# A convolutional decoder trunk on eight cores: the width-31 convolution computed for even and odd tokens at once

## The reference

```
h   = RMSNorm(x)
a_val, a_gate, z_a, gb, gc, hb, z_b = split(h @ w_in)          # 7 x 1024 columns
u   = a_val * sigmoid(a_gate)
ca  = causal depthwise conv, 31 taps, over u, + bias
ca  = LayerNorm of ca over the 128 channels of each of 8 heads
y_a = silu(ca) * silu(z_a)
v   = gc * hb
y_b = gb * (causal depthwise conv, 3 taps, over v) * silu(z_b)
x   = x + concat(y_a, y_b) @ w_out
```

## Time and profile before

| | us |
|---|---|
| median of 3 runs (1307.68 to 1352.38) | 1310.99 |
| the profiled execution | 1308.93 |
| span of its slowest core (core 2) | 1307.4 |
| spans of all eight cores | 1301.4 to 1307.4 |
| TensorE busy on it | 1220.8 |
| VectorE busy | 755.4 |
| ScalarE busy | 526.5 |
| GpSimd busy | 238.0 |

### The profile page before, as it was taken

How to read it: one execution, slowest core, us unless ns; L and a number is a source line. 1 busy time by engine, 2 the same in 40 slices (tenths; PEclk the granted TensorE clock), 3 DMA queues, 4 the chain that set the end, 5 groups by cost and what they waited for, 6 DMA issues and landing times.

```text
span 1307.4 us, 24848 instructions; the slowest of 8 cores (1301.4 to 1307.4 us)
## 1 busy us (share of the span) xinstructions
PE 1220.8 (93%) x8618; PEld 649.5 (50%) x8618; DVE 755.4 (58%) x1407; ACT 526.5 (40%) x764; POOL 238.0 (18%) x340
## 2 busy tenths in 40 slices
PE   4799999999899999999889999999999999999993
PEld 1355555555445555555445555544544555555541
DVE  2644456345666666667844445634476566666686
ACT  4677643767201101113537674367632111011252
POOL 0233323243010000000003333214230100100000
PEclk9999999999999999999999999999999999999997
DMA  9945431656143215230335553256441330422127
GB/s 245 197 92 107 104 73 37 126 113 119 17 96 55 34 26 92 34 52 13 41 78 123 101 105 72 51 106 125 88 49 24 52 49 8 65 33 33 17 107 168
DMA packets 89258, 102.09 MB, mean 78 GB/s; under 512 B 17008, under 2 KB 70384, under 8 KB 89072
## 3 DMA queue, kind: packets, MB, share of 16 engines
q0 software_dynamic: 20736, 37.76, 20.4%
q1 hardware_dynamic: 67584, 58.67, 18.5%
q10 hardware_dynamic: 816, 4.08, 0.9%
HBM read 92.41 MB, written 13.37 MB: 81 GB/s over the span
## 4 chain that ended last, share of the span: by engine, by line
PE 76%; DVE 6%; ACT 6%; issue 4%; DMA 4%; POOL 2%; SPq 1%; DVEq 0%; ACTq 0%; POOLq 0%
PE ps L327 66%; PE ps L442 7%; ACT sq L346 3%; DMA rep<-ubuf 2%; DVE x_sb L393 2%; PE ps L455 1%; DVE x_sb L379 1%; DMA x_sb<-xT 1%; PE ps L335 1%; POOL sq L425 1%; SPq L541 1%; PE ps L353 1%; DVE h_sb L371 1%; ACT L471 1%; DVE acc L665 1%
## 5 line engine op out<-in xcount | busy, mean ns | idle before, releaser
L327 PE MATMUL ps<-h_sb,wsl 128*128 128x424 bf16 (+1 forms) x4400 | 819.2, 342 | 2.0 <-ACT th_t L549 1.3
L327 PEld LDWEIGHTS ps<-h_sb,wsl 128*128 128x128 bf16 x4400 | 426.1, 98 | 363.9 <-issue 19.9
L327 PE MATMUL ps<-y_sb,wsl 128*128 128x424 bf16 (+1 forms) x1280 | 237.2, 342 | 15.9 <-DVE x_sb L393 15.9
L309 POOL DMA_DIRECT2D wsl<-w_in_r x112 | 60.1, 540 | 720.7 <-PE ps L327 507.8
L393 DVE TENSOR_TENSOR x_sb<-x_sb,ps 128x424 f32<-128x424 f32 (+1 forms) x320 | 175.4, 589 | 19.0 <-PE ps L327 8.8
L327 PEld LDWEIGHTS ps<-y_sb,wsl 128*128 128x128 bf16 x1280 | 123.9, 98 | 123.1 <-issue 22.7
L631 ACT ACTIVATE sz_t<-ps 128x424 f32<-128x424 f32 (+1 forms) x80 | 41.9, 523 | 303.4 <-PE ps L327 281.5
L556 DVE SCALAR_TENSOR_TENSOR ubuf<-th_t,ps 128x424 bf16<-128x424 f32 (+1 forms) x80 | 46.5, 583 | 180.5 <-PE ps L327 134.9
L442 PE MATMUL ps<-rep,wc 128*32 128x424 bf16 (+1 forms) x2560 | 119.7, 338 | 9.8 <-DMA rep<-ubuf 9.8
L665 DVE SCALAR_TENSOR_TENSOR acc<-ubuf,cw_b_sb,acc 128x424 f32<-128x424 bf16 (+1 forms) x192 | 112.8, 588 | 20.4 <-DVE acc L662 0.5
L647 DVE TENSOR_TENSOR ubuf<-ps,th_t 128x424 bf16<-128x424 f32 (+1 forms) x80 | 46.9, 586 | 130.5 <-PE ps L327 124.8
(11 more groups left out here) (50 smaller groups left out, 707.5 us busy)
## 6 DMA issues: line engine op xcount, KB each, us to landing
rep<-ubuf SPq DMA_DIRECT2D x256, 113.0 KB, 2.9
wsl<-w_in_r POOLq DMA_DIRECT2D x112, 256.0 KB, 5.3
wsl<-w_out_r POOLq DMA_DIRECT2D x32, 256.0 KB, 5.3
x_sb<-xT SPq DMA_DIRECT2D x16, 424.0 KB, 13.2
y_fm<-x_sb SPq DMA_DIRECT2D x16, 424.0 KB, 2.7
rep<-ubuf SPq DMA_DIRECT2D x64, 95.0 KB, 2.5
hista<-hist_a SPq DMA_DIRECT2D x16, 255.5 KB, 4.4
oa_copy<-sa_orig ACTq DMA_DIRECT2D x2, 1664.0 KB, 11.2
```

The lines of the kernel that those rows point to most:

```text
L309: P.op("pool", (lambda e, i=i, s=s: e.dma_start(out=wsl[:, s, :], in_=wseq[i])), reads=list(gate), writes=[w_r[s]], chan=ch_w[s], name=f"w ...
L327: ins = e.matmul(bank(bk, n), lhsT=l_, rhs=r_, start=(i == 0), stop=(i == len(pairs) - 1))
```

## The change

The tokens are reordered ahead of the launch: block 0 holds the even and block 1 the odd tokens of the first 848, blocks 2 and 3 those of the next 848, and block 4 the even, then the odd ones of its 352 prompt tokens, then the decode tokens. `ubuf` has a row of even and a row of odd tokens.

A convolution is now made for a group: blocks 0 and 1, blocks 2 and 3, or block 4 alone. `rep` has eight tiles; a tile's 128 rows are 16 channels x 2 phases x 4 shifts, and a matmul of 32 columns gives 16 channels x 2 phases. `a_copy` still issues four DMAs for each of blocks 0 to 3, now each from 128 partitions to 16, and eight for block 4. `st_conv` does a group in two banks (h = 0, 1), four passes each, over 424 columns (176 for block 4), and then casts both banks. `st_mean` takes channels and phases apart again and takes the mean away: two matmuls on `cb` with `um` for each block, four for block 4. `ones_n` is gone.

The order is changed too. `pipe` goes by the block number b: the group of blocks 0 and 1 is convolved in step 3 (banks 4 and 5), that of blocks 2 and 3 in step 0 of the next head (banks 4 and 5), block 4 in step 2 of the next head (banks 6 and 7). Their Ln and Exp come in steps 4 and 1; those of block 4 go with step 4. The output block of head 4 of group A comes one step later, the last in head 5. In group B the taps and the product of blocks 0 to 3 wait for the next step (`b_pend`), `out_norm(b - 2)` stands inside `b_step(b)` from b = 2 on, and the output blocks 3 and 4 of heads 3 and 7 follow `b_step(4)`. `rep` has two buffers (four before), `rstd_t` three and shared with the RMSNorm's, `sz_t` six with fixed places. `um` is one more load at the start, the taps of layer 1 are loaded in group B of layer 0, and the returned rows of u and v of the prompt are written in two pieces.

```diff
+HP = 16
+HQ = NPL // 2
+QN = SEQ // 2
...
+NM = 4
+NT = 8
+RW = BW + 4 * (NM - 1)
+NR = 2
...
+    ubuf = sb("ubuf", [128, 2, UQ], BF16)
     vbuf = ubuf
+    vsam = sb("vsam", [128, VSW], BF16)
...
+    rep = sb("rep", [128, NR, NT, RW], BF16)
     wsl = sb("wsl", [128, NW, 1024], BF16)
-    wc = sb("wc", [128, 2, 4 * NG, 32], BF16)
+    wc = sb("wc", [128, 2, NM * NT, 32], BF16)
+    um = sb("um_sb", [128, 4, 128], BF16)
...
+    def st_conv(gp, banks):
+        ms, rp, n = gp["j"] % 2, gp["rep"], gp["n"]
+        gp["bd"] = banks
+        for h in range(2):
+            def fn(e, h=h):
+                ins = None
+                for m in range(NM):
+                    for q in range(4):
+                        t = 4 * h + q
+                        off = 4 * (NM - 1 - m)
+                        ins = e.matmul(psum[32 * q:32 * q + 32, banks[h], 0:n], lhsT=wc[:, ms, NM * t + m, :], rhs=rep[:, rp, t, off:off + n],
+                                       start=(m == 0), stop=(m == NM - 1), tile_position=(0, 32 * q), skip_group_check=True)
+                return ins
+            P.op("pe", fn, reads=[wc_r[ms], rep_r[rp]], writes=[bank_r[banks[h]]])
+        for h in range(2):
+            P.op("dve", (lambda e, h=h: e.tensor_copy(cb[:, h, 0:n], bank(banks[h], n))), reads=[bank_r[banks[h]]], writes=[cb_r[h]])
+        for i, s in enumerate(gp["sts"]):
+            s["bd"] = banks[i]
+
+    def st_mean(gp, i):
+        s, n = gp["sts"][i], gp["n"]
+        bd, single = s["bd"], len(gp["sts"]) == 1
+        nb = BLOCKS[s["b"]][1]
 
         def fn(e):
             ins = None
-            for m in range(NG):
-                for q in range(4):
-                    w = wc[:, ms, 4 * m + q, :]
-                    ins = e.matmul(psum[32 * q:32 * q + 32, bd, 0:npr], lhsT=w, rhs=rep[:, rp, q, 4 * m:4 * m + npr],
-                                   start=(m == 0), stop=False, tile_position=(0, 32 * q), skip_group_check=True)
+            for p in ((0, 1) if single else (i,)):
+                c = n * p if single else 0
+                for h in range(2):
+                    ins = e.matmul(psum[:, bd, c:c + n], lhsT=um[:, 2 * h + p, :], rhs=cb[:, h, 0:n],
+                                   start=(h == 0 and c == 0), stop=(h == 1), skip_group_check=True)
+            if single:
+                ins = e.matmul(psum[:, bd, NPL:nb], lhsT=cmat16[:], rhs=cbs[:], start=False, stop=True, skip_group_check=True)
             return ins
...
+    def st_var_mm(s, bk):
+        nb = BLOCKS[s["b"]][1]
+        mm_group(bk, nb, [(ones_v[:], d2[:, s["d2"], 0:nb])], reads=[d2_r[s["d2"]], ones_r])
+        s["vb"] = bk
+
+    def st_rstd(pair, single):
+        ops = []
+        if pair:
+            vb, n = pair[0]["vb"], BLOCKS[pair[0]["b"]][1]
+            for t, s in enumerate(pair):
+                s["rstd"], s["rstd_r"] = rstd_t[:, t, 0:n], rstd_r[t]
+            ops.append((rstd_t[:, 0:2, 0:n], psum[:, vb:vb + 2, 0:n], [bank_r[vb], bank_r[vb + 1]], rstd_r[0:2]))
+        for s in single:
+            nb = BLOCKS[s["b"]][1]
+            s["rstd"], s["rstd_r"] = rstd_t[:, 2, 0:nb], rstd_r[2]
+            ops.append((rstd_t[:, 2, 0:nb], bank(s["vb"], nb), [bank_r[s["vb"]]], [rstd_r[2]]))
+        for o, i, rd, wr in ops:
+            P.op("act", (lambda e, o=o, i=i: e.activation(out=o, in_=i, func=AF.Ln, bias=LN_EPS)), reads=rd, writes=wr)
+        for o, i, rd, wr in ops:
+            P.op("act", (lambda e, o=o: e.activation(out=o, in_=o, func=AF.Exp, scale=-0.5)), reads=wr, writes=wr)
...
+    q_conv, q_y, hold = [], [], []
+    cur = {}
+
+    def pipe(at, b):
+        if at == 0:
+            gp = None
+            if q_conv and q_conv[0]["at"] == b:
+                gp = cur["g"] = q_conv.pop(0)
+                st_conv(gp, (6, 7) if b == 2 else (4, 5))
+            if b % 2 == 0:
+                while q_y:
+                    st_y(q_y.pop(0))
+            if b == 0 and "s" in cur:
+                st_tt(cur["s"])
+            if b == 3 and "s" in cur and gp is None:
+                st_var_mm(cur["s"], 7)
+                st_rstd([], [cur["s"]])
+        gp = cur.get("g")
+        if at == 1:
+            if b == 3 and "s" in cur and gp is not None:
+                st_var_mm(cur["s"], 7)
+            if b in (0, 2, 3) and gp is not None:
+                st_mean(gp, 0)
+            if b == 2 and gp is not None:
+                cur["s"] = cur.pop("g")["sts"][0]
+            if b == 0 and "s" in cur:
+                st_silu(cur["s"])
+            if b in (1, 4) and gp is not None:
+                for i, s in enumerate(gp["sts"]):
+                    st_var_mm(s, (6 if b == 1 else 2) + i)
+                st_rstd(gp["sts"], [cur["s"]] if b == 4 and "s" in cur else [])
         if at == 2:
-            while q_tt:
-                s = q_tt.pop(0)
-                st_tt(s)
-                q_silu.append(s)
-        elif at == 3:
-            while q_silu:
-                s = q_silu.pop(0)
-                st_silu(s)
-                q_y.append(s)
+            if b in (0, 3) and gp is not None:
+                st_mean(gp, 1)
+            if b == 0 and "s" in cur:
+                st_y(cur.pop("s"))
+            if b in (1, 4) and gp is not None:
+                for s in gp["sts"]:
+                    st_tt(s)
+            if b == 3 and gp is None and "s" in cur:
+                st_tt(cur["s"])
+        if at == 3:
+            if b in (1, 4) and gp is not None:
+                for s in cur.pop("g")["sts"]:
+                    st_silu(s)
+                    q_y.append(s)
+            if b == 3 and gp is None and "s" in cur:
+                st_silu(cur["s"])
+                q_y.append(cur.pop("s"))
...
+        last = b == NB - 1
+        n = HQ if last else BW
+        q0 = BW * (b // 2)
+        rn = n + 4 * (NM - 1)
+        if b % 2 == 0:
+            hold.append({"l": st["l"], "j": st["j"], "sts": [], "n": n, "rep": rot_rep.next(), "at": (3, 0, 2)[b // 2]})
+        gp = hold[0]
+        gp["sts"].append(st)
+        rp = gp["rep"]
+        for i in ((0, 1) if last else (b % 2,)):
+            for sh in range(4):
+                off = HP - 15 + q0 + sh
+                P.op("sp", (lambda e, i=i, sh=sh, off=off: e.dma_start(
+                    out=rep[64 * i + 16 * sh:64 * i + 16 * sh + 16, rp, :, 0:rn], in_=ubuf[:, i, off:off + rn])),
+                    reads=[u_r[b], (u_r[2 * (b // 2) - 2 + i] if b > 1 else pad_r)],
+                    writes=[rep_r[rp]] if b % 2 == 0 and i == 0 and sh == 0 else [], chan=ch_rep[rp])
         rep_r[rp].w = P.ops["sp"][-1]
+        if last or b % 2:
+            q_conv.append(hold.pop())
...
     def a_sz(st):
         n = BLOCKS[st["b"]][1]
         bz = st["banks"][2]
-        st["sz"] = isz = rot_sz.next()
+        st["sz"] = isz = st["b"] if st["b"] < NB - 1 else NB - 1 + st["j"] % 2
         P.op("act", (lambda e: e.activation(out=sz_t[:, isz, 0:n], in_=bank(bz, n), func=AF.Silu)),
              reads=[bank_r[bz]], writes=[sz_r[isz]])
-        q_conv.append(st)
 
     def a_state(l, j, b, slots):
         g = j * NB + b
-        return {"l": l, "j": j, "b": b, "g": g, "slots": slots, "bd": 4 + (g + 2) % 4,
-                "banks": (1, 2, 3) if g % 2 else (0, 1, 0)}
+        return {"l": l, "j": j, "b": b, "g": g, "slots": slots,
+                "banks": ((2, 3, 1), (0, 2, 3), (1, 0, 2), (3, 1, 2), (0, 1, 0))[b]}
 
...
+    b_pend = []
+
+    def b_taps(st):
+        l, j, b, isz = st
+        jj, n = j % 4, BLOCKS[b][1]
+        c0 = BLOCKS[b][0]
...
+        if last:
+            a3 = ac[:, 0:NPL].rearrange("r (p q) -> r p q", p=2)
+            rd = [u_r[2], u_r[3], u_r[4]]
+            seq = [(a3, vbuf[:, :, q0 - 1:q0 - 1 + HQ], 0), (a3, vbuf[:, :, q0:q0 + HQ], 2),
+                   (ac[:, 0:HQ], vbuf[:, 1, q0 - 1:q0 - 1 + HQ], 1), (ac[:, HQ:NPL], vbuf[:, 0, q0:q0 + HQ], 1)]
+            seq += [(ac[:, NPL:n], vsam[:, NS * k:NS * k + NSD], k) for k in range(WB)]
+        else:
+            p, e0 = b % 2, 2 * (b // 2)
+            rd = [u_r[e0], u_r[e0 + 1]] + ([u_r[e0 - 2], u_r[e0 - 1]] if e0 else [vpad_r])
+            o1 = q0 if p else q0 - 1
+            seq = [(ac[:, 0:n], vbuf[:, p, q0 - 1:q0 - 1 + n], 0), (ac[:, 0:n], vbuf[:, 1 - p, o1:o1 + n], 1),
+                   (ac[:, 0:n], vbuf[:, p, q0:q0 + n], 2)]
+        for i, (o, v, k) in enumerate(seq):
+            wcol = cw_b[:, l, j, k:k + 1]
+            creads = [vs_r, vh_r] if i >= 4 else rd
...
         proj(s_gb, b, bgb)
         P.op("dve", (lambda e: e.tensor_tensor(out=sz_t[:, isz, 0:n], in0=bank(bgb, n), in1=sz_t[:, isz, 0:n], op=ALU.mult)),
              reads=[bank_r[bgb], sz_r[isz]], writes=[sz_r[isz]])
         if g is not None:
-            pipe(2, g)
+            pipe(2, b)
+        if mid is not None:
+            mid()
+        if g is None:
+            bgc, bhb = [pool_all.next() for _ in range(2)]
         proj(s_gc, b, bgc)
         igc = rot_th.next()
```

(46 more changed lines are left out.)

268 lines of the change are left out of this document (105 added, 163 removed).

## The result

The changed kernel took 1384.22 us in the median (four executions, 1377.71 to 1386.78), the kernel before, timed beside it on the same chip, 1311.53 us. The ratio is 1.0557, with a 95% interval of 1.0506 to 1.0608. The forecast was 1321 us in a range of 1290 to 1345: it was wrong, by 63 us. In some executions one die of the chip shows a lower granted clock and takes longer; ratios and intervals here are of the others alone, while a median counts every execution. The profiled execution took 1385.28 us with a span of 1383.7 us, the one before it 1308.93 and 1307.4: the trace has 76.3 us to explain.

The account below looks back on a forecast made before the run. TensorE, busy for 1220.8 of 1307.4 us, was taken as the bound. Terms -38 - 7 + 25 + 7 + 12 + 10 + 1 = +10 on 1308.9 gave 1319, the median 2 above: 1321 us, range 1290 to 1345.

Parts of the forecast that it names:

- TensorE's work, -38 us: Group A's convolution and mean on TensorE: -55.8 for shorter convolution, +3.6 for starts, +14.4 for the mean, together -38 us.
- Waits that go, -7: TensorE's waits for casts and decode-token sums: 4.3 of 6.3 us and 2.5 us go, -7 us.
- `rep` stays at 9.8: Group A's convolutions: TensorE's wait for copies into `rep` stays at 9.8 us, as a group needs both blocks' copies.
- third rival: Copies into `rep`, writing 16 partitions, land late: at 5.8 us, waits add 24 us, giving 1345 us; chance 0.20.
- my estimate of 3.5: Landing of a 109 KB copy into `rep`: 1.05 us for 0.35 by port bandwidth, landing at 3.5, inside the cover.
- The head boundary, +25: First convolution of the next head waits for `st_tt` to free banks 4 and 5: 12 x 1.95 + 1.5 = +25 us.
- Group B, +29: New TensorE waits in group B, both layers: +7 us in head 0, +12 in head 3, +10 in head 7.
- The granted clock, "1.00, which leaves nothing to explain": Windows of the profile before: TensorE's granted clock is 1.00; the forecast's sum has no term for it.
- Rivals 1 and 2: First: no head-boundary wait, 1296 us, chance 0.15. Second: neither that nor group B's waits, 1267 us, chance 0.08.
- signs that I named for being wrong: In the profile after: a convolution line above 80 us, `rep` waits above 20, or no `tt_t` waits.

Follow-up runs that it names:

- e9: Label not defined in the text given; apparently the changed kernel with free banks, odd taps in their own step, late convolution and 128-partition copies into `rep`: 1318.62 us.
- e1: The changed kernel with each copy into `rep` written to all 128 partitions of one tile instead of 16 partitions of eight: 1351.29 us.

## Why the prediction was wrong, point by point

**TensorE's work, -38 us: right.** -38.3 at full clock. The convolution was to take 63.9 us and 3.6 for its starts; it took 75.2 with the clock falls in it, and 65.1 in the run where least clock was lost in it (e9). A pass of 176 columns takes 0.79 / 8 = 0.099 us, where I had 0.125:

```profile
270.55 0.79 PE L447 MATMUL ps<-rep,wc 128*32 128x176 bf16 x32
```

**Waits that go, -7: wrong by 4.** The sums of the decode tokens went, 2.5 us. The casts stayed at 6.2: the long ones behind the history's multiply are gone, but block 4's casts stand behind two `st_tt` on VectorE (one pair of casts starts at 272.81, as the `st_tt` end), and its mean waits up to 0.8 us for them, twelve times.

**"`rep` stays at 9.8": the step that failed.** It was 36.8, and 27 us of idle time and a good part of the falls hang on it. I had the point from which it decides (landing in 4.2 us) and priced the case as the third rival at +24; I gave it 0.20 and left it there. Beside it stood my estimate of 3.5 from figures of the Trainium skill (SBUF — State Buffer, "Door 1: The DMA port swizzle"). The median of all copies, 3.6, would even seem to bear that out. But the first pair's convolution waits for the last of eight copies, and those of block 1, behind two weight tiles, landed in 6.2 us in the median. In the kernel before they took 4.5 (5.6 in the head shown above), already more than my 4.2; I had set 2.8, the median of all copies, against it. Where a wait hangs on the latest of many transfers, the median of all is the wrong row. In the second layer six of the `rep` waits were 2.3 to 5.1 us; the one of 5.15 ends at 713.75 (there VectorE was late too: it finished the layer's first norms before u of block 1), and the clock behind it is in the windows above.

**The head boundary, +25: right.** 20.1 for `tt_t` in eleven pieces up to 1.9; two of the thirteen were taken by longer waits for `rep`. With the copies early (e1) it is 24.3 in thirteen. One of them, the 1.92 us between the last projection of step 4 and the convolution of the next head:

```profile
286.81 2.98 PE L332 MATMUL ps<-h_sb,wsl 128*128 128x416 bf16 x16
291.71 1.62 PE L447 MATMUL ps<-rep,wc 128*32 128x424 bf16 x32 [1.92 <-DVE tt_t L502]
```

The wait of 3.4 us for `sz_t` is not one of these: it stands at the first convolution of layer 0.

```profile
56.72 1.61 PE L447 MATMUL ps<-rep,wc 128*32 128x424 bf16 x16 [3.42 <-ACT sz_t L623]
```

**Group B, +29: right in size.** From one head's first silu of z to the next head's, both layers together, TensorE's idle time grew by 8.4 us in head 0, 12.9 in head 3 and 10.8 in head 7 with the end of the layer, 32 in all, where I had 7, 12 and 10; in the other heads of group B it grew by nothing. Head 0: the wait at block 4 grew from 1.63 to 4.72, by 3.1 where I had 2.8. Head 3: output block 3 waited 3.9 us where I had 3.7. Head 7: 2.4 to 2.5 ahead of an output block.

```profile
396.19 5.37 PE L332 MATMUL ps<-y_sb,wsl 128*128 128x416 bf16 x16 [4.72 <-DVE x_sb L398]
...
511.32 14.38 PE L332 MATMUL ps<-y_sb,wsl 128*128 128x424 bf16 x64 [3.88 <-DVE y_sb L697]
...
673.24 9.68 PE L332 MATMUL ps<-y_sb,wsl 128*128 128x424 bf16 x44 [2.46 <-DVE y_sb L697]
```

**The granted clock, "1.00, which leaves nothing to explain": the second step that failed, and the larger one.** It was 1.00 because TensorE hardly waited. Three rows of the trace before already had falls behind waits of 2.4 to 3.1 us (its 3 falls, 3.5 us); the windows that I read the earlier trace rows hold none of them. I priced each new wait at its length; most of those above 2 us cost 1.7 to 3.4 us on top. Here that is +33.7. The Trainium skill (TensorE: Matmul & The Clock Gate, "HAM oscillation — how this bites in real kernels") says that a wait for data inside a kernel throttles the clock again, each time. The traces agree for waits near 4 us: 16 of 16 added ones had a fall behind them. I should have weighed that page against the change and did not.

The sum with both put right: 1321 + 27 (`rep`) + 34 (clock) = 1382, for 1384 measured. Rival 3 was the case that happened, though its landing of 5.8 us was reached from 4.5 and not from 2.8; its 1345 lacked the clock too. Rivals 1 and 2 did not occur. One of the signs that I named for being wrong did show: `rep` waits above 20.

What stays open: by what mechanism fewer destination partitions make a copy land later; what else than the length of a wait decides whether the clock falls; and whether a better order of group B's first head would bring some of the last twenty us.

## What to carry to other kernels

On an engine that is busy for 93% of the time, work removed is not time removed: each cut of the work moves every deadline of the other engines and queues earlier by as much, so go through the list of waits that are nearly due, not only those that exist. If a wait hangs on transfers, take the landing of those very transfers, with what is issued ahead of them, from the trace. Price a new TensorE wait with the clock that falls behind it: in this kernel nearly each one above 3 us, and most above 2.2, cost its length and 1.7 to 3.4 us. When the list of waits blames a cast or a sum, look at what stands ahead of it in that engine's queue; twice here it was a load issued too late.

## What the runs showed of the hardware

- The granted clock falls to half (1.2 for 2.4 GHz) for some 3.4 us, at times twice that, behind an idle stretch of TensorE: sixteen waits of 3.8 to 4.2 us put into a stretch at 1.00 gave sixteen falls, and 32 of 2.0 to 2.4 us gave nineteen. With useless matmuls in some of the waits, nine falls were left of twenty.
- A copy of 109 KB from 128 partitions lands, in the median, in 3.9 us when it writes 16 partitions, 3.3 for 32, 2.8 for 64 and 2.4 for 128.
- With two weight tiles of 256 KB issued right ahead, such copies to 16 partitions landed in 6.2 us in the median; with the tiles moved away the same ones landed in 3.8.
- A matmul of 32 output columns and 176 moving ones costs, four side by side, 0.099 us a pass, just over half of the 0.20 for 424.
